# The running sum of the output's squares: GpSimd in SBUF instead of VectorE in PSUM

## The reference

```
h = rmsnorm(x, norm_gain)                     # x: 1024 x 2048
proj = h @ w_in                               # columns for three groups of heads
ya, yb, yc = hgrn2(...), band_attention(...), retention(...)   # each times silu(gate)
y = concatenate([ya, yb, yc])                 # 1024 x 2048
x = x + y @ w_out                             # w_out: 2048 x 2048
return x * rsqrt(mean(x * x, axis=-1) + eps) * final_gain
```

## Time and profile before the change

| | |
|---|---|
| median of three runs | 1789.12 us |
| profiled execution, time | 1785.92 us |
| its span | 1784.1 us |
| TensorE busy | 1744.6 us, 98% |
| VectorE | 1218.6 us, 68% |
| ScalarE | 669.6 us, 38% |
| GpSimd | 778.8 us, 44% |
| bytes moved | 323.29 MB, mean 181 GB/s |

### The profile page before, as it was taken

How to read it: one execution, slowest core, us unless ns; L and a number is a source line. 1 busy time by engine, 2 the same in 40 slices (tenths; PEclk the granted TensorE clock), 3 DMA queues, 4 the chain that set the end, 5 groups by cost and what they waited for, 6 DMA issues and landing times.

```text
span 1784.1 us, 26920 instructions
## 1 busy us (share of the span) xinstructions
PE 1744.6 (98%) x10330; PEld 1440.9 (81%) x10330; DVE 1218.6 (68%) x1714; ACT 669.6 (38%) x972; POOL 778.8 (44%) x545
## 2 busy tenths in 40 slices
PE   7999999999999999999999999999999999999996
PEld 6888888888888777888888888888888877888874
DVE  7856666554678988887787356555655548777987
ACT  4423334333435244353343233333533223333442
POOL 4545444444455744444444333333333450355450
PEclk9999999999999999999999999999999999999998
DMA  7767777685987424333234332323433269678876
GB/s 254 231 226 256 242 233 263 218 270 181 304 264 249 160 78 125 90 87 121 88 84 125 103 108 95 107 88 92 149 105 119 88 223 361 219 241 262 286 232 223
DMA packets 160851, 323.29 MB, mean 181 GB/s; under 512 B 18378, under 2 KB 19151, under 8 KB 160724
## 3 DMA queue, kind: packets, MB, share of 16 engines
q1 hardware_dynamic: 146458, 276.52, 48.7%
q10 hardware_dynamic: 14266, 45.05, 7.3%
HBM read 275.35 MB, written 46.15 MB: 180 GB/s over the span
## 4 chain that ended last, share of the span: by engine, by line
PE 91%; DVE 5%; DMA 1%; issue 1%; ACT 1%; POOL 0%; SPq 0%; ACTq 0%; DVEq 0%; POOLq 0%
PE prj L813 34%; PE prj L792 31%; PE prj L1095 14%; PE mix L958 2%; PE mix L941 2%; PE mix L832 1%; PE mix L951 1%; DVE arena L2279 1%; PE mix L884 1%; DMA in_raw<-in_wi 1%; PE mix L911 1%; PE mix L914 1%; PE mix L900 1%; PE mix L989 1%; PE mix L1011 1%
## 5 line engine op out<-in xcount | busy, mean ns | idle before, releaser
L765 POOL TENSOR_SCALAR w_hi<-w_sum 128x512 fp32r<-128x512 f32 x124 | 201.9, 1629 | 498.9 <-DMA w_sum<-in_w 481.1
L792 PE MATMUL prj<-in_hi,w_hi 128*128 128x512 f32 x840 | 329.3, 392 | 10.0 <-DVE w_lo L1687 9.6
L792 PE MATMUL prj<-in_lo,w_hi 128*128 128x512 f32 x840 | 327.8, 390 | 0.0
L792 PE MATMUL prj<-in_hi,w_lo 128*128 128x512 f32 x840 | 327.8, 390 | 0.0
L813 PE MATMUL prj<-mv_hi,w_hi 128*128 128x512 f32 x928 | 300.3, 405 | 0.9 <-DVE mv_lo L1756 0.9
L752 POOL TENSOR_TENSOR w_sum<-in_raw,in_raw 128x512 f32<-128x512 f32 x150 | 200.2, 1335 | 212.6 <-PE prj L792 201.8
L813 PE MATMUL prj<-mv_lo,w_hi 128*128 128x512 f32 x928 | 288.1, 392 | 0.0
L813 PE MATMUL prj<-mv_hi,w_lo 128*128 128x512 f32 x928 | 286.3, 390 | 0.0
L813 PEld LDWEIGHTS prj<-mv_hi,w_lo 128*128 128x128 f32 x928 | 174.2, 188 | 38.7
L813 PEld LDWEIGHTS prj<-mv_lo,w_hi 128*128 128x128 f32 x928 | 174.1, 188 | 38.4
L792 PEld LDWEIGHTS prj<-in_hi,w_hi 128*128 128x128 f32 x840 | 158.2, 188 | 45.1 <-issue 10.1
(11 more groups left out here) (177 smaller groups left out, 2480.3 us busy)
## 6 DMA issues: line engine op xcount, KB each, us to landing
in_raw<-in_wi SPq DMA_DIRECT2D x360, 256.0 KB, 3.2
raws<-in_wo SPq DMA_DIRECT2D x184, 256.0 KB, 3.5
w_sum<-in_w SPq DMA_DIRECT2D x116, 256.0 KB, 3.0
arena<-z_scratch ACTq DMA_DIRECT2D x56, 512.0 KB, 3.9
y_in<-y_scratch SPq DMA_DIRECT2D x80, 256.0 KB, 4.6
z_scratch<-acc_in SPq DMA_DIRECT2D x60, 256.0 KB, 3.7
z_scratch<-stage SPq DMA_DIRECT2D x26, 512.0 KB, 4.2
x_even<-in_xT SPq DMA_DIRECT2D x44, 256.0 KB, 3.9
```

The costliest lines, as they stand in the source:

```text
L765: nc.gpsimd.tensor_scalar(w_hi[q][:], w_sum[q][:], 1.0, None, ALU.mult).then_inc(w_hi_done, 1)
L792: last = nc.tensor.matmul(out, wt[wslot(n)][:, i % GRAN, :], mv[j % 2][:, i, :], start=(i == 0 and wt is w_hi and mv is in_hi), stop=(i == ...
```

## The change

The running sums lie in SBUF (`sum_sq[n]`) from the start. The first square of each half is written there by ScalarE itself; every other one is added by GpSimd, in place. In GpSimd's queue the adds of step v's squares stand ahead of the weight sums of step v+3. VectorE's adds and copies are gone. The semaphore `fsq_added` counts 30 adds instead of 32 instructions, and its waits are counted anew. ScalarE's queue keeps its order.

```diff
+        def adds_before(q):
+            return len([e for e in range(q) if e not in first_square])
...
+            def add_squares_of(v):                      # GpSimd
+                for q, (at_step, p, c) in enumerate(squares):
+                    if at_step == v and q not in first_square:
+                        pool.wait_ge(fsq_ready, q + 1)
+                        if adds_before(q) > 0:
+                            pool.wait_ge(fsq_added, adds_before(q))
+                        nc.gpsimd.tensor_tensor(sum_sq[c[1]][:], sum_sq[c[1]][:], rstd[:, half(q % 2)], ALU.add
+                                                ).then_inc(fsq_added, 1)
+
             for n in range(first_sum, GRANULES):
+                if n % 2 == 0:
+                    add_squares_of(n // 2 - 3)
                 a, b = raw_of[n]
...
+            for v in range(STEPS - 3, STEPS + 1):
+                add_squares_of(v)
...
             def output_ss(n):                           # TensorE
-                pe.wait_ge(fsq_added, last_square[n] + 1)
+                pe.wait_ge(fsq_added, adds_before(last_square[n] + 1))
...
                 act.wait_ge(acc_done, v)                # ScalarE, square(q)
-                if q >= 2:
-                    act.wait_ge(fsq_added, q - 1)
-                nc.scalar.activation(rstd[:, half(q % 2)], acc(p, c), ACT.Square).then_inc(fsq_ready, 1)
+                if q >= 2 and adds_before(q - 1) > 0:
+                    act.wait_ge(fsq_added, adds_before(q - 1))
+                dst = sum_sq[c[1]][:] if q in first_square else rstd[:, half(q % 2)]
+                nc.scalar.activation(dst, acc(p, c), ACT.Square).then_inc(fsq_ready, 1)
...
-            def add_square(q):                          # VectorE, with its calls
-                dve.wait_ge(fsq_ready, q + 1)
-                if q > 0:
-                    dve.wait_ge(fsq_added, q)
-                out = sum_sq[c[1]][:] if q in last_square else mix[1][:, cols]
-                if q in first_square:
-                    new = nc.vector.tensor_copy(out, rstd[:, half(q % 2)])
-                else:
-                    new = tt(out, mix[1][:, cols], rstd[:, half(q % 2)], ALU.add)
-                new.then_inc(fsq_added, 1)
...
                     comb_add(idx)
-                add_squares_of(v - 1)
                 for idx in combs_at(v):
                     comb_low(idx)
...
-            add_squares_of(STEPS - 1)
-            add_squares_of(STEPS)
             scale_half(0, 0, KB)
```

More of the change, by code:

```diff
@@ L2255, in accumulate @@
                 last.then_inc(acc_done, 1)
-            def add_square(q):
-                v, p, c = squares[q]
-                dve.wait_ge(fsq_ready, q + 1)
-                if q > 0:
-                    dve.wait_ge(fsq_added, q)
-                cols = half(c[1])
-                out = sum_sq[c[1]][:] if q in last_square else mix[1][:, cols]
-                if q in first_square:
-                    new = nc.vector.tensor_copy(out, rstd[:, half(q % 2)])
-                else:
-                    new = tt(out, mix[1][:, cols], rstd[:, half(q % 2)], ALU.add)
-                new.then_inc(fsq_added, 1)
[L2270 to L2273, removed]
             def scale_half(n, first, end):
```

## The result

The changed kernel takes 1790.18 us (median of 11 runs, 1787.61 to 1793.25). The kernel before, 11 runs with the first three among them, takes 1783.99. The ratio is 1.0029 with a 95% interval of 1.0018 to 1.0041, some 5.2 us slower. A second series gave 1.0032 (1.0019 to 1.0044). That is within the 0.5% that the prediction took for no change, but it is clear of the noise. The prediction was 1796.5 us; the forecast difference was +7.5.

A forecast was written before the change was run, and what follows sets the result against it. TensorE was taken to bound the output stage, with 2.4 us lost at step 48 to a late VectorE. Terms 0.4 + 4.8 + 2.5 - 0.15 = +7.5 us on 1789.1 gave 1796.6, stated as 1796.5; range 1786 to 1801.5.

The forecast's parts named there:

- up to step 40: Output stage: five one-square turns of 5.69 us make step 40 (40th output product tile) start at 1674.1, not 1673.69: +0.4.
- step 40 to 48: Output stage, two-square steps: five turns of 6.98 us make step 48 start at 1724.4, 4.8 us later than before.
- clock: Behind step 48's new wait TensorE's granted clock falls and matmuls slow: +2.5 us, limits 0 and 3.
- tail: End of kernel: last accumulation up to 0.7 us earlier, last add 1.29 instead of 0.70: -0.15 us, between -0.7 and +0.6.
- The ring: Output stage, once per step: square, adds, sums, w_hi, next square; 6.98 us with two squares. Forecast case, 42 in 100.
- the insertion: VectorE's pair sum goes between GpSimd's two adds in a two-square step and lengthens the turn by 0.60 us.
- The single-square ring: Same loop in steps with one square: 5.69 us a turn with the pair sum, 5.09 without.
- The lower limit of +1.6 at step 48: Step 48 starts at 1721.2 if two-square turns take 6.46 us, with no pair sum between the adds.
- Rival B: Pair sum not put between the adds, two-square turn 6.46 us: +4.0, 1793.1 us; 20 in 100.
- C: TensorE's clock stays up because the wait is broken into pieces: +5.0, 1794.1 us; 13 in 100.
- D: Every GpSimd operation takes the mean of 1.42 us, adding at steps 40 and 48: +12, 1801 us; 13 in 100.
- E: Squares come early enough, VectorE's relief wins, the 2.4 us wait at step 48 goes: 1786.6 us; 12 in 100.

The follow-up runs named there:

- the filler: Changed kernel plus 13 matmuls of no use ahead of step 48, to shorten TensorE's idle time there: 1790.57 us, 1.0024 to the kernel before.
- the run without adds: Changed kernel with each GpSimd add replaced by a one-column memset, same place and waits, sum of squares left out: 1780.63 us, 0.9977 to the kernel before.
- the ring without reading: Changed kernel, order and waits kept, each GpSimd add replaced by a write-only 128x1536 memset: 1788.55 us, 1.0028 to the kernel before.
- the run that only writes: Changed kernel with each GpSimd add replaced by a 128x1536 memset that waits for no square: 1781.52 us, 0.9980 to the kernel before.
- half adds: Changed kernel with each GpSimd add over 256 of its 512 columns, order and waits kept: 1781.52 us, 0.9982 to the kernel before.
- split: Squares' adds shared: VectorE keeps singles up to step 50 and firsts of two, GpSimd adds the others behind the weight sums: 1783.08 us, 0.9991 to before.
- behind: Changed kernel with step v's adds queued on GpSimd behind both weight sums of step v+3, not ahead: 1790.53 us, 1.0033 to the kernel before.
- without waits: Changed kernel with 30 full-size GpSimd adds on two idle SBUF tiles, waiting for no square: 1788.75 us, 1.0022 to the kernel before.

## Where the prediction was right, and where it failed

**The number and its level.** 1790.18 lies in the range of 1786 to 1801.5. Of the 6.3 us by which it was missed, 5.1 are the level: I added a difference to the median of three runs, 1789.12, while 11 runs give 1783.99. The profiled execution itself took 1785.92, a sign in plain sight that I noted as "3.2 above it" and didn't use. Had the difference been set on that, the forecast would have been 1793.4. The sign of the change was right, its size 7.5 for a measured 5.2 (ratio) to 6.2 (medians). I gave 0.73 to "the same", on the ground that 8.9 us is about what a measurement of this kernel tells from no change. That ground was wrong: the interval over 11 runs each is about 2 us to either side, and 5.2 us stand clear of it.

**Place by place**, from the two profiled executions:

| term | forecast | measured | how |
|---|---|---|---|
| up to step 40 | +0.4 | +1.0 | step 32 to 40: 44.85 (1628.31 to 1673.16) for 43.81 |
| step 40 to 48 | +4.8 | +3.7 | 49.61 for 45.90 |
| clock | +2.5 | +1.8 | 18.38 for 16.58 |
| tail | -0.15 | -1.1 | end of TensorE's products to the end of the span: 18.8 (from 1769.25) for 19.8 (from 1764.28) |
| sum | +7.5 | +5.5 | spans differ by 3.9, as step 32 started 1.6 earlier, ahead of any change |

- The ring was the likeliest case, and it is there, with the pair sum between the adds as foretold: 6.76 us for a forecast of 6.98. The mis-sized terms are the GpSimd operations (1.25 from start to start; I had 1.29, its duration, four times) and the insertion (0.45; I had 0.60); with these sizes the sum is 6.67, and 0.09 stays unassigned. Five turns of 0.22 are the 1.1 us that the term of step 48 was too high.
- The single-square ring was 5.69 and measured 5.5 to 5.6; step 40 waited 1.05 us all the same. Its y parts also landed late in this run (a DMA of 5.85 us in the chain ahead of it), so this term isn't clean.
- The wait ahead of step 48 was 2.1 us before, not 2.4: the row shows 0.30 us of work in its 2.40, and 43.77 us over eight steps are 5.47 a step, not 5.44. The lower limit of +1.6 at step 48 doesn't follow from its terms either; 1685.49 + 5 x 6.46 + 3.29 + 0.73 is 1721.8, +2.2. Neither touches the forecast of +4.8.
- Tail: I had missed that the two ones matmuls, 2.09 us at half clock before, might meet full clock. They took 1.14 here, and that is nearly all of the -1.1. It was luck: the changed kernel with the filler had 2.8 us of idle ahead of them as well, and there they took 2.09.
- Rival B (no insertion) and C (clock stays up) are refuted by rows of the changed kernel. D (every operation 1.42) didn't come in the ring, where the sums took 1.29. E's relief is real, some 2.3 us up to the end of the products in the run without adds, and was outweighed.

**The step that failed** is the sentence "so the work as such fits: in a two-square step 4 x 1.29 = 5.2 of 5.44 us. What doesn't fit is the order." The work doesn't fit: with VectorE's three turns at SBUF it is 6.4 us (6.36 and 6.47 measured), and the kernel with its order mended is as slow, 1.0033 to 1.0029. I had both pieces, a GpSimd pair that a VectorE instruction had stretched and a mean w_lo of 0.986, and used them for one instruction within the ring. I didn't add up all that takes turns in a step. The number came out near since the ring is there as well, and its turn, 6.76, is just longer than that sum; that the second cause didn't show in it was luck. Someone who had acted on my explanation, and moved the adds behind, would have gained nothing.

**The filler** missed as well. I took the cost of the clock to hang on the length of the last idle piece. The runs show otherwise (below).

What stays open: why step 32 started 1.6 us earlier in the changed kernel's profiled execution (it is less than the spread between runs), and how much of step 40's wait is the late y parts' and how much the ring's.

## What to carry to other kernels

Before moving work to GpSimd, add up for one step of the bounding engine all GpSimd instructions that read SBUF and a turn for every VectorE instruction with two SBUF inputs, not only GpSimd's own time; if the sum is over the step, the order of the queue alone won't save it. Then look for the ring apart from that: an instruction placed ahead of what it indirectly waits for needs a turn shorter than the step too, or one so little longer that the lateness of all its turns fits into the room there is (5.84 for 5.44 us cost little here). And set a forecast on the run from which its durations are taken, or on many runs, not on the median of three.

## What the runs showed of the hardware

- **Taking turns at SBUF.** A GpSimd add of 128x512 costs 1.25 us from start to start. A VectorE instruction with two SBUF inputs costs GpSimd 0.45, but itself up to 1.1 (1.78 us in place of 0.69): it waits for nearly a whole GpSimd instruction. GpSimd memsets of about 1.4 us cost VectorE nothing: beside them a pair sum took 0.70 in the ring without reading, and two w_lo 1.28 in the run that only writes. The pair sum of that run still met the weight sums (1.15 to 1.69).
- **TensorE's clock.** The three steps behind step 48 take 16.58 to 16.61 us where its wait was 2.1 us or less (before, half adds, writes only, split). They take 18.1 to 18.8 where it was 3.0 or more (behind 3.0, ring without reading 4.3, the changed kernel 5.0, without waits 5.5). So the price is 1.5 to 2.2 us, and doesn't grow with the wait: it was least behind the longest (18.08 us behind 5.5). The granted clock in the changed kernel, in pieces from the last matmul of step 47 on (the third number from the end of a row):

```profile
1717.80:1719.00 1.20, 0.00 (x0) 0.00 (x0) 1.05 (x2) 0.78 (x2) 0.39 (x1) 1.00 0.20 75
1719.00:1721.00 2.00, 0.00 (x0) 0.00 (x0) 2.00 (x3) 0.89 (x2) 1.41 (x2) 0.69 0.40 150
1721.00:1722.77 1.77, 0.00 (x0) 0.03 (x1) 0.96 (x2) 0.60 (x1) 1.77 (x2) 0.50 1.05 353
1722.77:1725.00 2.23, 2.23 (x5) 1.80 (x6) 0.69 (x1) 0.74 (x2) 2.09 (x2) 0.50 0.15 56
1725.00:1727.00 2.00, 2.00 (x7) 1.58 (x6) 1.70 (x3) 1.56 (x3) 0.88 (x1) 0.60 0.16 41
1727.00:1729.00 2.00, 2.00 (x11) 1.64 (x10) 0.00 (x0) 0.00 (x0) 1.86 (x3) 1.00 1.04 325
...
1769.30:1772.00 2.70, 0.00 (x0) 0.00 (x0) 0.68 (x1) 0.63 (x1) 1.26 (x1) 1.00 0.50 185
```

  It is at 0.50 (1.2 GHz of 2.4) before TensorE resumes and for some nine matmuls after. But the wait's length alone doesn't decide. With the filler 2.07 us of idle were followed by a drop, and before 2.10 us weren't. In the tail an idle piece of 2.8 us left it at 1.00 in the changed kernel, and one of 2.9 had let it fall before. With the filler the same 2.8 us were followed by two matmuls at half clock, and with half adds 2.2 us were (2.09 us each time), so what sets it isn't found here:

```profile
1772.29 2.09 PE mix L1136 x2
```
